# Two experts worked on together at the start of each expert layer, and routing rearranged

## What is computed

```python
x = layer_norm(ALPHA * x + m, ln1_g[layer], ln1_b[layer])
f = moe(x, w_router, b_router, moe_w1[layer], moe_w3[layer], moe_w2[layer])
...
logits = (xf @ w_router + b_router).astype(jnp.float32)
probs = jax.nn.softmax(logits, axis=-1)
pg = probs.reshape(t, N_EXPERT_GROUPS, EXPERTS_PER_GROUP)
group_score = lax.top_k(pg, TOP_K)[0].sum(-1)
g_sel = jnp.argmax(group_score, axis=-1)
...
hb = jax.nn.silu(xb @ w1[e]) * (xb @ w3[e])
return hb @ w2[e]
```

## Time and profile before

| | us |
|---|---|
| median of 3 runs | 1777.9 (1777.67 to 1778.08) |
| the profiled execution | 1778.61 |
| its span | 1777.4 |
| PE busy | 1708.9 (96%) |
| PE's weight loads | 1114.8 (63%) |
| DVE busy | 790.3 (44%) |
| ACT busy | 625.0 (35%) |
| POOL busy | 121.9 (7%) |
| DMA queue q1: 542.14 MB | 76.0% of 16 engines' span |

### The profile page before, as it was taken

The page is one execution under the profiler, slowest core; times in us unless marked ns, Lnnn a source line. Parts: engine busy times, 40 slices in busy tenths (PEclk is TensorE's granted clock), DMA queues, the critical chain, the costliest instruction groups (busy, mean ns, idle before and its releaser), DMA issues.

```text
span 1777.4 us, 23957 instructions
## 1 busy us (share of the span) xinstructions
PE 1708.9 (96%) x10000; PEld 1114.8 (63%) x10000; DVE 790.3 (44%) x1510; ACT 625.0 (35%) x1201; POOL 121.9 (7%) x143
## 2 busy tenths in 40 slices
PE   9999999998989989999999989999999999999998
PEld 8974344433334974444343333887999899789986
DVE  6961111111103782111111012866888677668875
ACT  5541110100002661000100001666666564656664
POOL 0000000000000000000000000131111001401100
PEclk9999999999999999999999999999999999999999
DMA  9759999999999789999999999533555544335550
GB/s 392 308 226 358 403 428 428 428 429 426 426 426 419 288 320 365 429 428 429 427 429 427 425 427 419 181 140 135 176 188 182 197 166 145 141 131 174 183 190 24
DMA packets 55941, 544.90 MB, mean 307 GB/s; under 512 B 6289, under 2 KB 6289, under 8 KB 8337
## 3 DMA queue, kind: packets, MB, share of 16 engines
q1 hardware_dynamic: 55440, 542.14, 76.0%
q10 hardware_dynamic: 384, 1.13, 0.2%
HBM read 542.19 MB, written 1.05 MB: 306 GB/s over the span
## 4 chain that ended last, share of the span: by engine, by line
PE 67%; DMA 20%; DVE 7%; ACT 3%; issue 1%; POOL 1%; SPq 0%; ACTq 0%; DVEq 0%
PE PS L1208 23%; DMA ring<-in_w 20%; PE PS L410 12%; PE PS L412 11%; PE PS L411 11%; DVE wl L393 2%; PE PS L1188 2%; PE PS L1262 2%; PE PS L925 1%; ACT wh L387 1%; PE PS L1224 1%; PE PS L1276 1%; PE PS L1371 0%; DVE F L1060 0%; PE PS L1330 0%
## 5 line engine op out<-in xcount | busy, mean ns | idle before, releaser
L1208 PE MATMUL PS<-ring,F 128*64 128x512 f32 x2072 | 462.0, 595 | 28.5 <-DMA ring<-in_w 23.6
L393 DVE TENSOR_TENSOR wl<-ring,wh 128x512 fp32r<-128x512 f32 x504 | 362.9, 738 | 166.6 <-ACT wh L387 163.9
L387 ACT ACTIVATE wh<-ring 128x512 fp32r<-128x512 f32 x504 | 314.5, 630 | 271.7 <-PE PS L412 251.3
L1208 PEld LDWEIGHTS PS<-ring,F 128*64 128x64 f32 x2072 | 146.2, 137 | 322.0 <-issue 279.3
L410 PE MATMUL PS<-xh,wl 128*128 128x256 f32 x1144 | 329.7, 288 | 2.4 <-DVE wl L393 2.3
L411 PE MATMUL PS<-xl,wh 128*128 128x256 f32 x1144 | 323.5, 283 | 0.0
L412 PE MATMUL PS<-xh,wh 128*128 128x256 f32 x1144 | 323.5, 283 | 0.0
L410 PEld LDWEIGHTS PS<-xh,wl 128*128 128x128 f32 x1144 | 219.2, 192 | 5.6 <-DVE wl L393 2.4
L411 PEld LDWEIGHTS PS<-xl,wh 128*128 128x128 f32 x1144 | 219.3, 192 | 0.7
L412 PEld LDWEIGHTS PS<-xh,wh 128*128 128x128 f32 x1144 | 219.3, 192 | 0.0
L410 PE MATMUL PS<-wh,xl 128*128 128x512 f32 x352 | 142.6, 405 | 6.4 <-DVE xl L555 3.5
(11 more groups left out here) (405 smaller groups left out, 1909.5 us busy)
## 6 DMA issues: line engine op xcount, KB each, us to landing
ring<-in_w SPq DMA_DIRECT2D x100, 2048.0 KB, 25.6
ring<-in_w SPq DMA_DIRECT2D x65, 1024.0 KB, 11.4
ring<-in_ffn_up SPq DMA_DIRECT2D x44, 1024.0 KB, 4.9
early<-in_w SPq DMA_DIRECT2D x16, 2048.0 KB, 27.3
F<-in_w SPq DMA_DIRECT2D x16, 2048.0 KB, 28.6
ring<-in_ffn_down SPq DMA_DIRECT2D x22, 1024.0 KB, 4.9
F<-in_w SPq DMA_DIRECT2D x20, 1024.0 KB, 8.1
ZX<-in_w SPq DMA_DIRECT2D x8, 2048.0 KB, 28.7
```

The source lines that it names most:

```text
L387: act.e.activation(self.wh[:, p % NPIECE, :], self.piece_source(p), ACT.Copy).then_inc(*self.up("w_hi", p))
L393: dve.e.tensor_tensor(self.wl[:, p % NPIECE, :], self.piece_source(p), f32(self.wh[:, p % NPIECE, :]), ALU.subtract).then_inc(*self.up("w_ ...
L1208: t = pe.e.matmul(PS[64 * half:64 * half + 64, bank, :], lhs(k), weights[:, a:a + 512], start=(k == 0), stop=(k == 7))
```

## The change

**Order of the loads.** `FIRST_PAIR` brings the first 24 chunks as 0, 12, 1, 13, 2, 14, 3, 15, then 4 to 7, 16 to 19, 8 to 11, 20 to 23, with chunk 7 still in its own late place. The rule that gives out the slots afterwards is not touched.

**The pair.** PE makes the first product of both experts together: two blocks of the gather, each copied out alone, then the chunk of expert 0 and the chunk of expert 1 that use them, four times. The second product of expert 0 and half of that of expert 1 follow, the transposes for expert 0, the other half, the third product of expert 0, the gather of the next pair, the transposes for expert 1, and its third product. Expert 1 has PSUM banks 1 and 2 for its products, and a place of its own for its silu.

**Routing.** ACT takes one more quarter of the norm (with a second scalar from POOL), and features are divided 9 to 7 between ACT and DVE. The logits of the two halves of the tokens go to PSUM partitions 0 to 15 and 64 to 79 of two banks, and their matmuls alternate; the router's bias is loaded twice. The ranks of both halves come from one matmul of 32 columns and one of 16 in place of three.

The core of the diff:

```diff
+FIRST_PAIR = ([12 * ex + c for c in range(4) for ex in range(2)] +
+              [12 * ex + 4 * w + c for w in (1, 2) for ex in range(2) for c in range(4)])
...
-        LOAD_ORDER[m + 7:m + at + 1] = LOAD_ORDER[m + 8:m + at + 1] + [m + 7]
+        pair = [m + i for i in FIRST_PAIR if i != 7]
+        LOAD_ORDER[m:m + 24] = pair[:at] + [m + 7] + pair[at:]
...
-        if h == 0:
-            dve.e.tensor_scalar(sm[:, 505:506], mv[:, 0:1], -1.0, None, ALU.mult).then_inc(*self.up("less_mean", stage))
+        if h == 0 or stage in ROUTED:
+            a = 506 if h else 505
+            dve.e.tensor_scalar(sm[:, a:a + 1], mv[:, 0:1], -1.0, None, ALU.mult).then_inc(*self.up("less_mean", stage, h))
...
+        for d in range(1 if stage in ROUTED else 2):
...
+        if stage in ROUTED:
+            pool.wait_ge(self.at("rstd", (stage, 1)), self.at("less_mean", stage, 1))
+            pool.e.tensor_tensor(sm[:, 507:508], sm[:, 506:507], sm[:, 501:502], ALU.mult).then_inc(
+                *self.up("shift1", stage))
...
+    def scalar_norm_last(self, stage):
+        sm = self.sm
+        src, ready = self.norm_source(stage, 1, 1)
+        self.act.wait_ge(self.at("shift1", stage), ready)
+        self.act.e.activation(self.norm_buffer(stage)[:, 1, 512:1024], src, ACT.Identity, scale=sm[:, 501:502],
+                              bias=sm[:, 507:508]).then_inc(*self.up("norm1_last", stage))
...
+        for h in range(2):
+            e.dma_start(self.brt[64 * h:64 * h + 16, :], A["b_router"]).then_inc(self.s_br, 16)
...
+        return v["hh"] if ex > 1 else v["Y"][0] if ex else self.F[:, 768:1280]
...
+        for k in range(3):
+            self.scalar_route_feature(layer, 0, k)
+        self.scalar_norm_last(ROUTED[layer])
+        self.scalar_route_feature(layer, 0, 3)
+        for k in (0, 1, 2, 3, 7):
+            self.scalar_route_feature(layer, 1, k)
...
+        for h in range(2):
+            dve.wait_ge(self.at("turned", f"route{layer}", h, 1))
+            for k in range(4, 8 - h):
+                dve.e.tensor_scalar(self.RT[:, k, h * 128:h * 128 + 128], self.turned_bank(h, k), g[:, k:k + 1],
+                                    b[:, k:k + 1], ALU.mult, ALU.add).then_inc(*self.up("xt_odd", layer, h, k))
...
+    def logits_of(self, h):
+        return self.PS[64 * h:64 * h + 16, 2 * h, 0:128]
...
-        self.tensor_logits(layer, 0, range(4))
+        for k in range(3):
+            self.tensor_logits(layer, 0, k)
         self.tensor_route_turn(layer, 1)
-        self.tensor_logits(layer, 0, range(4, 8))
-        self.tensor_logits(layer, 1, range(8))
+        for i, k in enumerate((0, 1, 4, 2, 5, 6, 3, 7)):
+            if i < 5:
+                self.tensor_logits(layer, 0, i + 3)
+            self.tensor_logits(layer, 1, k)
         order, ready = self.TURN_ORDER, (lambda h, k: self.route_feature(layer, h, k))
-        frees = [[at("logits_t", layer)], [], [], []]
...
-        pe.e.matmul(PS[:, 4, 0:16], self.upper[:, :], M[:, 0, :], start=True, stop=True)
-        pe.e.matmul(PS[:, 4, 16:32], self.ones[:, 0:128], M[:, 0, :], start=True, stop=False)
-        pe.e.matmul(PS[:, 4, 16:32], self.upper[:, :], M[:, 1, :], start=False, stop=True).then_inc(*up("ranked", layer))
+        pe.e.matmul(PS[:, 4, 0:32], self.upper[:, :], self.sm[:, 192:224], start=True, stop=False)
+        pe.e.matmul(PS[:, 4, 16:32], self.ones[:, 0:128], M[:, 0, :], start=False, stop=True).then_inc(*up("ranked", layer))
...
+        for h in range(2):
+            t = pe.e.matmul(self.first_gathered_of(k), self.X[:, h, k * 128:k * 128 + 128], v["S"][:, h, :],
+                            start=(h == 0), stop=(h == 1))
+        t.then_inc(*self.up("gathered", layer, 0, k))
...
+    def first_bank(self, ex, w):
+        return (4 + w) if ex == 0 else (1 + w)
...
+    def tensor_first_product(self, layer):
+        pe, PS, xg = self.pe, self.PS, self.moe_views()["xg"]
+        for c in range(4):
+            for kk in range(2):
+                self.tensor_first_gather(layer, 2 * c + kk)
+            for ex in range(2):
+                n = CHUNK[f"moe{layer}"] + 12 * ex + c
+                weights = self.chunk(n)
+                pe.wait_ge(self.landed(n), self.at("ranks_read", layer))
+                for kk in range(2):
+                    k = 2 * c + kk
+                    pe.wait_ge(self.first_gathered(layer, k))
+                    for half in range(2):
+                        a = kk * 1024 + half * 512
+                        t = pe.e.matmul(PS[64 * half:64 * half + 64, self.first_bank(ex, 0), :],
+                                        xg[:, k, ex * 64:ex * 64 + 64], weights[:, a:a + 512], start=(k == 0), stop=(k == 7))
+                t.then_inc(*self.up("expert_chunk", n))
+    def tensor_first_pair(self, layer):
+        pe, at, v = self.pe, self.at, self.moe_views()
+        slots = [(lambda k, ex=ex: v["xg"][:, k, ex * 64:ex * 64 + 64]) for ex in range(2)]
+        hidden = (lambda k: v["hT"][:, k % 4 * 128 + k // 4 * 64:k % 4 * 128 + k // 4 * 64 + 64])
+        self.tensor_first_product(layer)
+        pe.wait_ge(at("counts_read", layer))
+        self.tensor_product(layer, 0, 1, self.first_bank(0, 1), slots[0])
+        self.tensor_product(layer, 1, 1, self.first_bank(1, 1), slots[1], range(2))
+        self.tensor_turn_hidden(layer, 0)
+        self.tensor_turn_gates(layer, 0)
+        self.tensor_product(layer, 1, 1, self.first_bank(1, 1), slots[1], range(2, 4))
+        pe.wait_ge(at("hid_t", layer, 0))
+        self.tensor_product(layer, 0, 2, 5, hidden)
+        self.tensor_gather(layer, 1, 0)
+        self.tensor_turn_hidden(layer, 1)
+        self.tensor_gather(layer, 1, 1)
+        pe.wait_ge(at("hid_t", layer, 1), at("y0", layer, 0), at("y1", layer, 0))
+        self.tensor_product(layer, 1, 2, 5, hidden)
...
+        for k in (0, 2, 4, 6):
+            act.wait_ge(self.at("gathered", layer, 0, k))
+            act.e.activation(self.moe_views()["xg"][:, k, :], self.first_gathered_of(k), ACT.Copy).then_inc(
+                *self.up("xg0", layer, *((0,) if k > 5 else (0, k))))
...
+    def scalar_first_pair(self, layer):
+        act, at, up, PS, v = self.act, self.at, self.up, self.PS, self.moe_views()
+        for ex in range(2):
+            act.wait_ge(self.expert_done(layer, ex, 0))
+            if ex:
+                act.wait_ge(self.expert_done(layer, 0, 1))
+            act.e.activation(self.silu(ex), PS[:, self.first_bank(ex, 0), :], ACT.Tanh, scale=0.5).then_inc(
+                *up("tanh", layer, ex))
+        act.wait_ge(at("hid_turned", layer, 0))
+        act.e.activation(v["hT"], PS[:, 4, :], ACT.Copy).then_inc(*up("hid_t", layer, 0))
+        act.wait_ge(at("gates_turned", layer, 0))
+        act.e.activation(v["Gt"], PS[:, 6, :].rearrange("p (h s t) -> p h s t", h=2, s=2), ACT.Copy).then_inc(
+            *up("gates_t", layer, 0))
+        act.wait_ge(self.expert_done(layer, 0, 2), at("hidden", layer, 1))
+        act.e.activation(v["Y"][0][0:64, :], PS[0:64, 5, :], ACT.Copy).then_inc(*up("y0", layer, 0))
+        self.scalar_gathered(layer, 1)
+        act.wait_ge(at("hid_turned", layer, 1))
+        act.e.activation(v["hT"], PS[:, 4, :], ACT.Copy).then_inc(*up("hid_t", layer, 1))
+        act.wait_ge(self.expert_done(layer, 1, 2))
+        act.e.activation(v["Y"][1][0:64, :], PS[0:64, 5, :], ACT.Copy).then_inc(*up("y0", layer, 1))
...
+    def vector_first_hidden(self, layer, ex):
+        self.dve.wait_ge(self.expert_done(layer, ex, 1), self.at("silu", layer, ex))
+        if ex:
+            self.dve.wait_ge(self.at("hid_turned", layer, 0))
+        self.dve.e.scalar_tensor_tensor(out=self.moe_views()["hh"], in0=self.silu(ex), scalar=0.5,
+                                        in1=self.PS[:, self.first_bank(ex, 1), :], op0=ALU.mult, op1=ALU.mult).then_inc(
+            *self.up("hidden", layer, ex))
...
+        self.vector_first_gathered(layer, 1)
+        self.vector_first_gathered(layer, 3)
+        self.moe_vector_gates(layer)
+        self.vector_first_gathered(layer, 5)
+        self.vector_first_gathered(layer, 7)
+        self.vector_pick(layer, 1)
+        self.vector_first_silu(layer, 0)
+        self.vector_first_hidden(layer, 0)
+        self.vector_first_silu(layer, 1)
+        self.vector_first_hidden(layer, 1)
+        self.vector_gate_slots(layer, 1)
+        dve.wait_ge(self.expert_done(layer, 0, 2))
+        e.tensor_copy(v["Y"][1][64:128, :], PS[64:128, 5, :]).then_inc(*up("y1", layer, 0))
+        self.vector_gathered(layer, 1)
+        dve.wait_ge(self.expert_done(layer, 1, 2))
+        e.tensor_copy(v["Y"][0][64:128, :], PS[64:128, 5, :]).then_inc(*up("y1", layer, 1))
```

More of the change, by code:

```diff
@@ L1190, in tensor_gather, with tensor_product @@
         t.then_inc(*self.up("gathered", layer, q, half))
-    def tensor_product(self, layer, ex, w, bank, lhs):
+    def tensor_product(self, layer, ex, w, bank, lhs, chunks=range(4)):
         pe, PS = self.pe, self.PS
```

(39 more changed lines are left out.)

88 lines of the change are left out of this document (40 added, 48 removed).

## The result

The changed kernel takes 1797.14 us (median of 5 runs, 1796.29 to 1798.95) against 1778.01 before: 1.0108 times as long, 95% interval 1.0098 to 1.0119, or 19.1 us slower. The profiled execution took 1797.11, its span is 1795.9.

A forecast was written before the change was run, and what follows sets the result against it. The continuous stream of expert loads was taken as the bound. Load 40 landing 5.7 us later in layer 0 and 8.3 in layer 1, plus 1.5 lag, made 15.5 on 1777.9: 1793.4 us, range 1787 to 1801.

The forecast's parts named there:

- wait of load 31 for chunk 8: Early in each expert layer, load 31 waits until chunk 8, now used seventeenth, frees its slot; 14 to 24 us slower, chance 0.84.
- When chunk 8 is used: TensorE's first expert pair: seventeen chunks, four gathers, switches and transposes put it 35.6 us after the gather's start, between 35 and 38.
- G: Start of the gather in each expert layer: 132.88 and 674.96 us before, forecast at 131.6 and 673.9.
- Routing: Before each gather: earlier features, overlapping logits and fewer rank rows start it 1.3 us sooner in layer 0, 1.1 in layer 1.
- The pause: Load queue between chunk 6's load and chunk 8's: empty for 7 to 8 us, some 28 to 36 us after the gather's start.
- From load 31's landing to load 40's: Load stream in layer 0: eight more loads at 2.45 us, then load 40, two chunks, 4.9 us.
- The mark in layer 0: Landing of load 40, whose shift moves the kernel's end: 190.8 us before, 196.5 to 198 forecast, 5.7 later without lag.
- the lag: Load stream just started: load 40 can land up to 1.5 us later per layer; half of that each, 1.5 together.
- Faster, loads in the order of use: Rival: slots follow use order, sixteen loads and load 40 run back to back; 9.6 and 7.0 us sooner, 1761.3; chance 0.04.
- No change: Rival: the load stream absorbs the delay, needing some 15 us of pauses after 190.8 and 730.5 us; chance 0.04.
- Slower still: Rival: TensorE stalls ahead of chunk 8, for instance every gather waiting 0.7 us more for its copy; 1803 us; chance 0.06.
- The other steps: Smaller copies on ACT and DVE, DVE's gating chain, second silu buffer, PSUM banks, second bias load: all hidden, no time added.

The follow-up runs named there:

- e8_one_group: Changed kernel with both halves' logits in PSUM partitions 0 to 15, so their alternating matmuls use the same TensorE column group; 1798.42 us, run once.
- e1_use_order: Changed kernel with load slots given on in the order in which chunks are used, not by lowest chunk number; 1774.54 us, ratio 0.9981.
- the kernel with singles: Changed kernel with slots given on in order of use and one chunk a load up to number 51 instead of 39; 1770.23 us, ratio 0.9956.
- e7_later_start: Changed kernel with six idle matmuls of 256 columns (2.8 us) ahead of the gather in each layer; 1803.32 us, ratio 1.0140.
- e2_route_only: Kernel before with the routing part of the change alone (norm, features, logits, ranks); 1775.81 us, ratio 0.9987.
- e3_pair_only: Changed kernel with the routing of before, keeping the pair and the order of loads; 1800.21 us, ratio 1.0126.

## Why the prediction was right, and where it was short

The forecast was 1793.4 us by a wait of load 31 for chunk 8; 1797.1 was measured, inside 1787 to 1801, by that wait.

*When chunk 8 is used.* Forecast 35.6 after G; load 31 was issued 35.75 after G in both layers. The first two-block gather with its wait takes 1.17 (131.81 to the product at 132.98), where I took 1.15, and the other three 1.10; the copy of one block is 0.28 us. Two chunks of products between gathers take 3.65 us, 0.19 more than twice 1.73, where I took 0.14. The parts make 35.75 with the 1.1 for transposes that I had assumed.

```profile
132.56 0.28 ACT L1493 ACTIVATE F<-PS 128x128 f32<-128x128 f32 x1 [2.70 <-PE PS L1398]
```

*Routing.* Forecast 1.3 and 1.1, measured 1.07 and 0.87. The last feature was ready at 125.7 as said; the logits ended at 126.44 and not at 126.0. The mechanism was right, and e8_one_group shows the assumption behind it. My argument for it was weaker than it looks: that rows are longer than their step doesn't prove it, since the mixer's fp32r rows, which use the whole array, are 0.39 long and follow each other every 0.23 us too. What speaks for it is the pace of float32 rows: 0.12 us each with 128 columns (24 in 2.79), 0.24 with 256 (12 in 2.86), and only 0.217 with the 512 columns of a product, where at that rate some 0.47 would be due (an estimate from the first two). The two terms are 0.5 too large together.

*The pause.* I had forecast 7 to 8 us with an empty queue. It was 5.6 in layer 0 (162.6 to 168.2, apart from the trickle) and about 5 in layer 1 (713.0 to 717.8), because the loads ahead of it were late: load 30 lands 33.9 and 31.4 us after G. That cost nothing, since load 31 lands 4.8 after its own issue in both layers. No step of the sum used the length of the pause.

*From load 31's landing to load 40's.* This is the term that was mis-sized. Forecast 19.6 for eight loads, measured 21.5 in layer 0 and 21.6 in layer 1: 0.25 of the difference because eight single chunks land 2.48 apart, not 2.45, and 1.7 because two loads behind the pause landed late (loads 32 and 34 in layer 0, 3.74 and 2.97 us behind their predecessors; loads 32 and 33 in layer 1, 3.96 and 2.68). I had seen such a lag in the earlier trace rows, 8.7 for a double load, and took half of 1.5 for each layer. It came whole and a little more in both, 3.5 us in all where the sum has 1.5.

*The mark in layer 0* was forecast at 196.5 to 198, and is 198.8; the one in layer 1 is 10.5 later by itself, where 8.3, and 9 with the lag, was forecast. The sum of the terms: 0.5 from routing, 0.5 from the pace, 2.0 from the lag and 0.3 from chunk 8 make 3.3 of the 3.6 us between 15.5 and 19.1.

*The rivals.* "Faster, loads in the order of use" was right as a mechanism that this kernel does not have: e1_use_order is it, but at 1774.5, not 1761.3. I had let load 40 run on with the sixteen before it. In layer 0 the two neighbouring slots that it takes there held chunks 20 and 21, so it waits for chunk 21 and lands 57.4 us after G, not 49.6; the kernel with singles, 1770.2, is closer. In layer 1 it waits for nothing late and still lands 53.3 after G: load 24 took 7.8 us from issue to landing where I had 4.8, and the others went at 2.50 where I had 2.45. "No change" fell with e7_later_start. "Slower still" needed copies 0.7 us late; they are not.

*The other steps hid, as said*: TensorE goes through the first pair in 52.1 us (131.8 to 183.9, from the timeline) with no idle stretch but those ahead of the products.

## What to carry to other kernels

When a kernel reorders the use of buffers, the rule that refills them must be reordered too: a queue that waits in order is as late as its latest wait, however many slots lie empty behind it. Look for the point from which the transfers never pause again; up to there every microsecond reached the end of this kernel, and behind it none was won in any run here. A saving on an engine that will catch up with its transfers anyway is worth only what it brings the releases forward while the stream starts. For the pair that is some 4 us in all, of a rearrangement of 52 us in each layer; the first release accounts for 0.8 a layer (load 24 goes out 3.14 us after G, and 3.96 before).

## What the runs showed that I had not expected

A double load (2 MB) that starts the stream again lands 8.6 to 8.7 us after its issue, three times in three kernels (before, e1_use_order, e2_route_only, each time load 40 of layer 0; load 39 lands 1.4 us ahead of its issue in e1_use_order and 0.8 to 0.9 behind it in the others). A single one into an empty queue, load 31, lands after 4.6 to 4.9. In a running stream doubles are 4.9 apart and singles 2.48, so 4.8 + 2.45 = 7.25 would be expected of the double.

And the stream that starts with load 31 loses time within its next eight loads: against a pace of 2.48 it is 1.7 and 1.8 us in the two layers of the changed kernel, and 1.3 to 2.9 in e3_pair_only, e7_later_start and e8_one_group. The trace has single packets of 8 KB there that took 1.8 us (at 174.2 in the changed kernel) and 1.9 (at 160.1 before) where 0.31 is the rule. That a few packets can hold up a load is seen at load 30 of the changed kernel: its stream is over at 162.6 but for single packets until 165.4, the trickle in the view above, and it lands at 165.8. Why packets are slow is open; no run was aimed at it.
